# Expert rows written to DRAM by indirect DMA, a ring of nine weight buffers, and the modulation of both layers in layer one

## The chip, the core and the metric

The kernel runs on one core of one Trainium2 chip. The metric is device microseconds of one execution, the median of several runs. All data are float32. TensorE (PE in the profile) runs at one of two granted clock levels: a granted clock of 1.00 is 2.4 GHz, 0.50 is 1.2 GHz.

## What is computed

One inference step of a two-layer backbone for 128 context tokens and 256 latent tokens, with a model width of 1024. The conditioning vectors give six modulation vectors per layer and stream (shift, scale and gate, for the mixer and for the experts). Each layer:

```python
mod = (silu(cond) @ w_mod + b_mod).reshape(6, 1024)
h = rms_norm(x, norm_mix) * (1 + mod[1]) + mod[0]
proj = h @ w_in                      # three head groups: short conv, attention, RWKV-7
x = x + mod[2] * (mixed(proj) @ w_out)
h2 = rms_norm(x, norm_ffn) * (1 + mod[4]) + mod[3]
# hierarchical MoE: best group of 4, best 2 of its 8 experts, 32 experts in all
y[t] = sum over the 2 chosen experts e of weight[t, e] * ((silu(h2 @ w1[e]) * (h2 @ w3[e])) @ w2[e])
x = x + mod[5] * y
```

At the end one more RMS norm. With 384 tokens and two experts each there are 768 (token, expert) rows in a layer, 24 for an expert on average.

## The kernel before

Layout: tokens are columns and the 1024 channels are 8 chunks of 128 partitions. One loop runs over the two layers, and inside it a loop over rounds of 64 slots for each expert; the trace holds one round per layer.

**Mixer** (`mixer_stage`, L400). SP issues every weight load from one queue, in program order, with waits in between. The modulation weights of a layer are 24 pieces of 1 MB, in two buffers (`mod_stream`): piece n+2 is issued by `load_mod` (L802) once TensorE has used piece n. Two pieces make a block of 512 outputs (`mod_piece`, matmuls in L430); a block is then copied by VectorE (L1079), turned by TensorE (`mod_turn`, L441) and summed (L1085). The first eight pieces stand ahead of the input projection. The other sixteen stand between its eleven column groups, two behind each of the first eight (`mod_with`, `MOD_WITH`). `project` (L481) computes one half of a column group: 16 matmul passes of 385 columns. TensorE executes in program order, so whatever it waits for in `mod_with` holds up the next `project`.

At the end of the mixer, when the last two chunks of the mixed heads are ready (`mix_ready`), SP loads the first three weight units of the experts (L822, L826). Meanwhile the last output projection (L669), the second norm, the router and the slot positions are computed, and the normed tokens are stored row by row to DRAM (`h2_rows`, L838). Then the block ends, SP clears all semaphores in a block of its own, and the number of rounds is read.

**Experts** (`experts_round`, L1478). Experts come in pairs (16 pairs), 64 slots each. A weight unit is one matrix of one expert, 2 MB; a pair has six, in six buffers, each loaded again when the pair's own step has used it (L1521). For a pair TensorE does: `up` (L1592, 64 passes of 512 columns for w1 and w3), in it the slot-to-token index (L1559), then `scatter` (L1599) of the pair before: a matmul with the one-hot weights that adds the results of 128 slots onto all 384 tokens, in banks 0 to 5, which are kept as sums through the round. Then the turned one-hot weights (L1616), the turned hidden rows (L1620), `down` (L1607, 32 passes) and the turned token rows of the next pair (L1567). GpSimd gathers these rows from `h2_rows` by an indirect DMA of 128 rows of 4 KB (L1725). After the last pair three weight units are loaded once more, for a possible next round.

**Between and behind.** The next mixer begins with adding the sums to the residual, from PSUM (`add_experts`, L394), and the same is done ahead of the final norm (`close_sums`, `final_stage`). Before the first mixer a block of its own loads the tokens and the constants (L1776 to L1783) and clears the sum banks.

Of the kernel before, what the change touches and what calls it, by code (L numbers as in the profile page):

```python
# [23 lines left out]
I32 = mybir.dt.int32  # L24
# [21 lines left out]
MAX_ROUNDS = T // SLOTS  # L46
DECAY = 0.6065306597126334
# [15 lines left out]
for _name, _w in (("ident", P), ("ones", P), ("heads", P), ("before", P), ("swap", P),  # L63
                  ("cos", TS), ("sin", TS), ("att", 2 * P), ("tri", 4 * P), ("level", 2 * LEVELS * P),
                  ("reset", 3 * 129), ("iota", SLOTS), ("rev", EPG), ("eps", 2), ("tokid", TILES)):
    CK[_name] = _n
    _n += _w
# [3 lines left out]
def build(nc, a, o):  # L71

    ctx = ExitStack()
    with ctx:
# [15 lines left out]
        par = sb("par", NPK)  # L90
        nout = sb("nout", KC)
        cond = sb("cond", 2 * KC)
        mod_sb = sb("mod_sb", 96)
        mod = mod_sb[:, :].rearrange("p (j s) -> p j s", s=2)
        gains = sb("gains", 32)
        gain = gains[:, :].rearrange("p (n c s) -> p n c s", n=2, s=2)
        posm = sb("posm", TILES * N_EXP)
        wall = sb("wall", TILES * N_EXP)
        rounds_i = sb("rounds_i", 1, I32)
        slot_tok = sb("slot_tok", 1, I32)  # L100
        h2_rows = nc.dram_tensor("h2_rows", (T, D), F32, kind="Internal").ap()
        AR_N = 45080
# [7 lines left out]
        def pk(name, i=0, n=1):  # L110
            return par[:, PK[name] + i:PK[name] + i + n]
# [14 lines left out]
        Pm, PT = arena[:, h_at:h_at + 768], arena[:, h_at + 768:h_at + 1536]  # L126
        slab = take(8 * W).rearrange("p (c w) -> p c w", c=8)
# [9 lines left out]
        mix_at = at[0]  # L137
        mixT = take(KC * T).rearrange("p (c t) -> p c t", c=KC)
# [4 lines left out]
        R_, K_, V_ = take(T), take(T), take(T)  # L143
# [17 lines left out]
        zeros = X_.rearrange("p i q -> p (i q)")[:, 0:512]  # L161
# [16 lines left out]
        rtw = take(KC * 36).rearrange("p (c e) -> p c e", c=KC)  # L178
# [6 lines left out]
        r_at = [h_at + KC * T + 24]  # L185

        def rt(n):
# [10 lines left out]
        oh2 = rt(TILES * EPG).rearrange("p (t e) -> p t e", t=TILES)  # L198
        tw = rt(TILES * EPG).rearrange("p (t e) -> p t e", t=TILES)
# [3 lines left out]
        assert r_at[0] <= mix_at  # L203

        unit = [arena[:, i * 4096:(i + 1) * 4096] for i in range(2)]
        h2tok = arena[:, mix_at:mix_at + TILES * D].rearrange("p (t d) -> p t d", t=TILES)
        assert 2 * 4096 <= mix_at  # L210
        m_at = mix_at + TILES * D
        unit = [arena[:, m_at + i * 4096:m_at + (i + 1) * 4096] for i in (2, 3)] + unit + \
               [arena[:, m_at + i * 4096:m_at + (i + 1) * 4096] for i in (0, 1)]
        m_at += 4 * 4096
        e_at = [2 * 4096]

        def moe(n):
            if e_at[0] + n > mix_at and e_at[0] < m_at:
                e_at[0] = m_at
            e_at[0] += n  # L220
            assert e_at[0] <= AR_N
            return arena[:, e_at[0] - n:e_at[0]]

        Sel = moe(TILES * P).rearrange("p (t j s) -> p t j s", t=TILES, j=2)
        Wsel = moe(TILES * P).rearrange("p (t j s) -> p t j s", t=TILES, j=2)
        WselT = moe(T)
# [3 lines left out]
        yg = moe(D)  # L230
        xtok = moe(D)

        pos3 = posm[:, :].rearrange("p (t e) -> p t e", t=TILES)
        wall3 = wall[:, :].rearrange("p (t e) -> p t e", t=TILES)
# [70 lines left out]
        N_MOD, N_IN, N_OUT = 2 * 6 * D // MC, IN_W // UC, D // UC  # L305
        SUM_BANKS = KC * T // 512
# [4 lines left out]
        MOD_WITH = [[m for m in range(N_MOD1, N_MOD) if (m - N_MOD1) * 8 // (N_MOD - N_MOD1) == k] for k in range(N_IN)]  # L311
# [66 lines left out]
        def segments(c):  # L378

            at_, out = c * T, []  # L380
            while at_ < (c + 1) * T:
                n = min((c + 1) * T, (at_ // 512 + 1) * 512) - at_
                out.append((at_ // 512, at_ % 512, at_ - c * T, n))
                at_ += n
            return out

        def add_experts(done=None):

            for c in range(KC):
                for bk, col, t0, n in segments(c):  # L390
                    for st, (cols, _) in enumerate(STREAMS):
                        lo, hi = max(t0, cols.start), min(t0 + n, cols.stop)
                        if lo < hi:
                            ins = nc.vector.scalar_tensor_tensor(  # L394
                                xT[:, c, lo:hi], bank[bk][:, col + lo - t0:col + hi - t0],
                                mod[:, 40 + c, st:st + 1], xT[:, c, lo:hi], ALU.mult, ALU.add)
                if done:
                    done(ins)

        def mixer_stage(layer):  # L400

            pr = PsumTurns(list(range(5)))
            att_turn = [0]

# [7 lines left out]
            with nc.Block() as block:  # L412
                @block.tensor
                def _(pe):
                    mm = nc.tensor.matmul

                    def piece(n):
                        pe.wait_ge(sem(f"piece_loaded{n % 2}"), 16 * (n // 2 + 1))
                        return stream[n % 2]
# [34 lines left out]
                    pe.wait_ge(sem("cond_ready"), 2)  # L454
                    for n in range(N_MOD1):
                        mod_piece(n)
                        if n % 2 and n > 1:
                            mod_turn(n // 2 - 1)
                        if 1 <= n <= KC // 2:
                            pe.wait_ge(sem("sq_ready"), 2 * n)  # L460
# [1018 lines left out]

# [430 lines left out]
```

## Time and profile before

| | us |
|---|---|
| median of three runs | 2093.07 (2092.96 to 2096.77) |
| profiled execution, device time | 2098.63 |
| its span, first to last instruction | 2096.7 |
| TensorE busy | 1846.2 (88%) |
| VectorE / ScalarE / GpSimd busy | 644.5 / 372.6 / 138.6 |
| moved by DMA | 524.84 MB, 250 GB/s over the span |
| mean granted clock | 0.957 |

Times below count from the start of the span. A timeline row reads: start, duration of the whole group, engine and line, operation, result<-operands, tile, number of instructions, and in brackets how long the engine stood idle before it and what ended that. A float32 matmul shows as two passes. "SPq" and "POOL" rows of DMAs show the issue, not the transfer. In a queue row the last figure is the share of the time of 16 DMA engines in that stretch.

### The profile page before, as it was taken

Reading aid. Unit: us, or ns where it says so; the run is one execution under the profiler, and the core shown is the slowest. Engines: PE = TensorE matmul, PEld = TensorE weight load, DVE = VectorE, ACT = ScalarE, POOL = GpSimd, SP = SyncE. Lnnn points to the kernel's source line nnn. Section 1 sums busy time; section 2 is a strip of 40 time slices with the busy share of each in tenths; the row PEclk is TensorE's granted clock in tenths of the full one; section 3 lists DMA queues with packets and bytes.
Section 4 is the critical chain, followed back from the end, with each engine's and each line's share of the span. In section 5 each row is a group of like instructions: output and inputs, shape, how many; then the busy total and the mean of one; then the engine's idle time right before and its main releaser. Section 6 shows DMA issues by size and latency. Waiting matters only on the chain. (4 is left out here: it accounts for less than half of the span.)

```text
span 2096.7 us, 25042 instructions
## 1 busy us (share of the span) xinstructions
PE 1846.2 (88%) x9550; PEld 1042.7 (50%) x9550; DVE 644.5 (31%) x1549; ACT 372.6 (18%) x733; POOL 138.6 (7%) x230
## 2 busy tenths in 40 slices
PE   6998878898899999999789997889879999999994
PEld 2556666675444344344335565677553434434432
DVE  3034566536111111111132436674441111111112
ACT  1022233212110111111021123331121011111101
POOL 0002021120000000000000111122000000000000
PEclk8999899999899999999979999999989999999997
DMA  8551000014899999999676300000259999999992
GB/s 331 211 217 49 16 1 1 16 36 156 352 425 427 425 428 425 418 420 425 269 292 250 141 36 16 1 1 16 90 208 417 427 426 427 426 424 423 420 422 104
DMA packets 48833, 524.84 MB, mean 250 GB/s; under 512 B 5616, under 2 KB 7664, under 8 KB 13808
## 3 DMA queue, kind: packets, MB, share of 16 engines
q1 hardware_dynamic: 42272, 506.00, 58.3%
q0 software_dynamic: 4320, 15.73, 1.9%
q10 hardware_dynamic: 2160, 2.03, 0.3%
q8 instruction: 50, 0.82, 0.2%
q14 instruction: 31, 0.25, 0.0%
HBM read 518.50 MB, written 5.24 MB: 250 GB/s over the span
## 5 line engine op out<-in xcount | busy, mean ns | idle before, releaser
L1592 PE MATMUL bank<-arena 128*64 128x512 f32 x2048 | 453.9, 595 | 0.9
L1592 PEld LDWEIGHTS bank<-arena 128*64 128x64 f32 x2048 | 146.0, 136 | 261.7 <-issue 261.0
L1607 PE MATMUL bank<-arena 128*64 128x512 f32 x1024 | 226.8, 594 | 22.5 <-ACT arena L1705 20.8
L481 PE MATMUL bank<-arena 128*128 128x385 f32 x704 | 239.7, 498 | 2.5 <-ACT arena L910 2.5
L481 PEld LDWEIGHTS bank<-arena 128*128 128x128 f32 x704 | 135.0, 195 | 94.8 <-issue 9.5
L1599 PE MATMUL bank<-arena 128*128 128x384 f32 (+2 forms) x768 | 174.9, 384 | 1.7 <-DVE arena L1689 1.7
L871 POOL TENSOR_TENSOR arena<-arena,const 128x256 f32<-128x256 f32 x168 | 108.1, 668 | 741.3 <-DVE arena L1227 573.0
L1599 PEld LDWEIGHTS bank<-arena 128*128 128x128 f32 x768 | 123.3, 190 | 59.8 <-issue 27.8
L1607 PEld LDWEIGHTS bank<-arena 128*64 128x64 f32 x1024 | 71.8, 135 | 157.0 <-issue 128.9
L1249 DVE TENSOR_TENSOR arena<-arena,bank 128x384 f32<-128x384 f32 x176 | 95.9, 553 | 146.7 <-PE bank L572 113.3
L1685 DVE TENSOR_TENSOR arena<-arena,bank 128x512 f32<-128x512 f32 x32 | 22.0, 688 | 337.9 <-PE bank L1592 337.9
L1689 DVE COPY arena<-bank 128x512 f32<-128x512 f32 x32 | 22.1, 692 | 250.8 <-PE bank L1607 250.8
L1725 POOL DMA_INDIRECT arena<-h_rows,slot_tok x30 | 28.4, 946 | 1044.3 <-DVE slot_tok L1682 1044.3
L572 PE MATMUL bank<-arena 128*128 128x128 f32 x480 | 74.2, 295 | 25.0 <-ACT arena L991 25.0
L574 PE MATMUL bank<-arena 128*128 128x128 f32 x576 | 85.9, 290 | 3.8 <-ACT arena L991 3.8
L669 PE MATMUL bank<-arena 128*128 128x384 f32 x256 | 86.2, 488 | 3.0 <-DVE arena L1399 3.0
L430 PE MATMUL bank<-arena 128*32 128x512 f32 x384 | 52.2, 648 | 37.1 <-DMA arena<-in_w_mod 26.9
L557 PE MATMUL bank<-arena 128*128 128x128 f32 x576 | 78.1, 280 | 6.7 <-issue 6.6
L1712 ACT ACTIVATE arena<-bank 128x384 f32<-128x384 f32 x32 | 15.7, 491 | 373.2 <-PE bank L1616 373.2
L1710 ACT ACTIVATE arena<-bank 128x512 f32<-128x512 f32 x32 | 19.1, 598 | 349.5 <-PE bank L1592 349.5
L574 PEld LDWEIGHTS bank<-arena 128*128 128x128 f32 x576 | 77.7, 205 | 4.7 <-ACT arena L991 4.2
L572 PEld LDWEIGHTS bank<-arena 128*128 128x128 f32 x480 | 64.9, 205 | 28.6 <-ACT arena L991 28.4
(251 smaller groups left out, 1808.2 us busy)
## 6 DMA issues: line engine op xcount, KB each, us to landing
arena<-in_exp_w SPq DMA_DIRECT2D x198, 2048.0 KB, 14.9
arena<-in_w_mod SPq DMA_DIRECT2D x48, 1024.0 KB, 5.3
arena<-in_w_in SPq DMA_DIRECT2D x22, 1024.0 KB, 8.3
arena<-in_w_out SPq DMA_DIRECT2D x8, 768.0 KB, 4.3
h_rows<-arena SPq DMA_DIRECT2D x2, 1536.0 KB, 5.3
const<-in_const SPq DMA_DIRECT2D x1, 2088.0 KB, 10.6
arena<-in_w_out_rw SPq DMA_DIRECT2D x2, 1024.0 KB, 4.7
x_sb<-in_xT SPq DMA_DIRECT2D x1, 1536.0 KB, 6.7
```

What stands on the lines that cost most here:

```text
L430: last = mm(mod_bank[0][32 * g:32 * g + 32, :], scond[:, 4 * second + g, :], mod_stream[n % 2][:, g, :], start=not second, stop=bool(second))
L481: last = mm(b[:, 0:W - 2], w[:, c, j * P:(j + 1) * P], hT[:, c, 1:W - 1], start=(c == 0), stop=(c == KC - 1))
L557: last = mm(b[:, (i % 3) * P:(i % 3 + 1) * P], Nl[lev % 2][:, i, :], X_[:, i, :] if lev else ident, start=True, stop=True)
L572: last = mm(o_, XT[:, i, :], T1[:, i, :], start=True, stop=True)
L574: last = mm(o_, T1[:, i, :], XT[:, i, :], start=True, stop=True)
L669: last = mm(b[:, 0:T], w[:, c - chunks[0], col:col + P], mixT[:, c, :], start=(c == chunks[0]), stop=(c == chunks[-1]))
L871: ins = g.tensor_tensor(Nl[lev % 2][:, 2 * t:2 * t + 2, :], G[:, t, :, 0, 0, :], m, ALU.mult)
L1249: L.free(tt(x[:, ii, :], x[:, ii, :], b[:, 0:T].rearrange("p (i q) -> p i q", i=3), ALU.add), pr, name, hold=False)
L1592: last = mm(b[HALF[j], :], Xg[:, c, j, :], unit[2 * m + j][:, c * DE:(c + 1) * DE], start=(c == 0), stop=(c == KC - 1))
L1599: mm(bank[bk][:, col:col + n], yg[:, c * P:(c + 1) * P], WselT[:, t0:t0 + n], start=False, stop=True, skip_group_check=True)
L1607: last = mm(b[HALF[j], :], hidT[:, f_, j, :], unit[4 + j][:, lo:lo + 512], start=(f_ == 0), stop=(f_ == FC - 1))
L1725: nc.gpsimd.indirect_dma_start(xtok, None, h2_rows[:, :], bass.IndirectOffsetOnAxis(ap=slot_tok[:, 0:1], axis=0))\
```

## The change

- Expert results are no longer added up in PSUM. They are scaled by their weight on the way out of PSUM, and GpSimd writes each slot's row to one of two rows of its token in DRAM (`y_rows`) by an indirect DMA; an empty slot has an index out of bounds and moves nothing. The `scatter` matmuls and the turned one-hot weights go. The two rows of every token are read back, added and turned (`read_rows`, `turn_rows`, `add_experts`) at the start of the next mixer and ahead of the final norm. `h2_rows` is stored twice, so that either row index of a token finds it.
- Weight units go through nine buffers in turn. The first nine of a layer are loaded from `mix_ready` on; unit n waits for the step that used unit n-9. A unit is loaded again for a further round only by an indirect DMA whose indices are out of bounds in the first round (`hold_again`). The first two input pieces of the next mixer are loaded behind the last unit.
- All 48 modulation pieces of both layers are used in the first layer: 8 ahead of the projection, and 40 behind the first eight column groups, six and four in turn. The second layer has none.
- The block ahead of the first mixer goes; its loads stand behind the first two modulation pieces. Layers and pairs are written out instead of looped; the mixer's semaphores are cleared inside the round.

```diff
-        MOD_WITH = [[m for m in range(N_MOD1, N_MOD) if (m - N_MOD1) * 8 // (N_MOD - N_MOD1) == k] for k in range(N_IN)]
+        MOD_WITH = [[m for m in range(N_MOD1, N_MOD) if (m - N_MOD1) // 2 * 8 // ((N_MOD - N_MOD1) // 2) == k] for k in range(N_IN)]
...
+        def read_rows(sp):
+            for t in range(TILES):
+                for k in range(2):
+                    sp.dma_start(ytok[:, t, k, :], y_rows[k * T + t * P:k * T + (t + 1) * P, :])\
+                      .then_inc(sem(f"rows_read{t}"), 16)
+
+        def turn_rows(pe, pr):
+            for t in range(TILES):
+                pe.wait_ge(sem("rows_added"), t + 1)
+                for half in range(2):
+                    b = pr.open(pe, f"rows{t}_{half}")
+                    for i in range(4):
+                        last = nc.tensor.transpose(b[:, i * P:(i + 1) * P],
+                                                   ytok[:, t, 0, (4 * half + i) * P:(4 * half + i + 1) * P], ident)
+                    pr.close(last, f"rows{t}_{half}")
...
+            add(0)
+            residual(0)
+            add(1)
+            add(2)
+            residual(1)
+            residual(2)
...
                     def mod_with(k):
-                        for m in MOD_WITH[k]:
+                        for m in MOD_WITH[k] if first else ():
...
-                    for n in range(N_MOD1):
-                        load_mod(n)
+                    if first:
+                        for n in range(N_MOD1):
+                            load_mod(n)
+                            if n == 1:
+                                sp.dma_start(x_sb[:, :], a["xT"]).then_inc(sem("x_loaded"), 16)
+                                sp.dma_start(const[:, :], a["const"]).then_inc(sem("const_loaded"), 16)
+                                sp.dma_start(nout[:, :], a["nout"]).then_inc(sem("stored"), 16)
+                    else:
+                        for s_ in range(HELD):
+                            sp.sem_clear(sem(f"held{s_}"))
+                        read_rows(sp)
                     for m, u in enumerate(IN_ORDER):
                         load(m, a["w_in"][bass.ds(layer * (N_IN * P) + u * P, P), :])
-                        for n in MOD_WITH[m]:
+                        for n in MOD_WITH[m - 1] if first and m else ():
                             load_mod(n)
...
+                    sp.wait_ge(sem("mix_ready"), 2)
+                    def hold(n):
+                        i, m, j = n // 6, n % 6 // 2, n % 2
+                        src = a[("exp_w1", "exp_w3", "exp_w2")[m]][bass.ds((layer * N_EXP + i * 2 + j) * P, P), :]
+                        sp.dma_start(unit[n], src).then_inc(sem(f"held{n}"), 16)
+                    for n in range(HELD - 1):
+                        hold(n)
+                    pr.filled(sp, f"out1_{KC - 1}")
+                    hold(HELD - 1)
                     pr.copied(sp, f"htok{TILES - 1}1")
-                    sp.dma_start(h2_rows.rearrange("(t p) d -> p t d", p=P), h2tok).then_inc(sem("h2_stored"), 16)
+                    for k in range(2):
+                        sp.dma_start(h2_rows[k * T:(k + 1) * T, :].rearrange("(t p) d -> p t d", p=P), h2tok)\
+                          .then_inc(sem("h2_stored"), 16)
+                    sp.wait_ge(sem("h2_stored"), 32)
...
+                    for n in range(HELD, 6 * PAIRS):
+                        i, m, j = n // 6, n % 6 // 2, n % 2
+                        before = n - HELD
+                        sp.wait_ge(sem(used[before % 6 // 2]), before // 6 + 1)
+                        sp.dma_start(unit[n % HELD], a[names[m]][bass.ds((layer * N_EXP + i * 2 + j) * P, P), :])\
+                          .then_inc(sem(f"x_unit{n % HELD}"), 16)
+                    if layer + 1 < DEPTH:
+                        sp.wait_ge(sem("x_down"), PAIRS - 1)
+                        for k in range(2):
+                            src = a["w_in"][bass.ds((layer + 1) * (N_IN * P) + IN_ORDER[k] * P, P), :]
+                            sp.dma_start(stream[k], src.rearrange("p (c n) -> p c n", c=KC)).then_inc(sem("x_next"), 16)
...
+                    index(0)
+                    turned(0)
+                    index(1)
+                    for i in range(PAIRS):
+                        up(i)
+                        turned(i + 1)
+                        turn_hidden(i)
+                        index(i + 2)
+                        down(i)
...
+                    hold_again(0)
+                    hold_again(1)
+                    gather(0)
+                    for n in range(2, HELD):
+                        hold_again(n)
+                    gather(1)
+                    for i in range(PAIRS):
+                        gather(i + 2)
+                        pool.wait_ge(sem("x_y0"), i + 1)
+                        pool.wait_ge(sem("x_y1"), i + 1)
+                        if i:
+                            pool.wait_ge(sem("x_put"), 16 * i)
+                        g.indirect_dma_start(y_rows[:, :], bass.IndirectOffsetOnAxis(ap=slot_idx[i % 3][:, 0:1], axis=0),
+                                             yg[i % 2], None, bounds_check=2 * T - 1, oob_is_err=False)\
+                            .then_inc(sem("x_put"), 16)
+                    pool.wait_ge(sem("x_put"), 16 * PAIRS)
```

## Rows read from the trace of the kernel before

**Rows 1.** The page, 40 slices of 52.4 us: busy tenths of the DMA engines.

```profile
DMA  8551000014899999999676300000259999999992
```

**Rows 2.** Timeline of TensorE, one pair of the first layer's experts.

```profile
596.53 3.66 PE L1592 MATMUL bank<-arena 128*64 128x512 f32 x16
611.57 5.47 PE L1599 MATMUL bank<-arena 128*128 128x384 f32 x24
619.29 7.09 PE L1607 MATMUL bank<-arena 128*64 128x512 f32 x32 [0.69 <-ACT arena L1705]
627.86 3.66 PE L1592 MATMUL bank<-arena 128*64 128x512 f32 x16
```

**Rows 3.** DMA queues in 560 to 1030 us: packets, MB, share.

```profile
q1 hardware_dynamic: 13086, 190.54, 95.8%
q0 software_dynamic: 2016, 7.34, 4.0%
q8 instruction: 3, 0.05, 0.0%
```

**Rows 4.** Weight units of the experts (L1521), 480 to 700 us, from issue.

```profile
DMA to landing us min/median/max: 8.6/17.8/23.7
```

**Rows 5.** Timeline of TensorE, the second column group of the first projection.

```profile
72.18 1.92 PE L430 MATMUL bank<-arena 128*32 128x512 f32 x16
74.03 0.66 PE L441 MATMUL bank<-const,arena 128*128 128x128 f32 x4
74.53 10.52 PE L481 MATMUL bank<-arena 128*128 128x385 f32 x32
```

**Rows 6.** Timeline of TensorE, modulation ahead of the first projection, and its first group.

```profile
32.71 1.06 PE L430 MATMUL bank<-arena 128*32 128x512 f32 x8 [0.53 <-DMA arena<-in_w_mod]
38.77 1.07 PE L430 MATMUL bank<-arena 128*32 128x512 f32 x8 [1.85 <-DMA arena<-in_w_mod]
46.37 13.48 PE L481 MATMUL bank<-arena 128*128 128x385 f32 x32 [1.27 <-ACT arena L910]
```

**Rows 7.** Modulation pieces (L802), 22 to 42 us, from issue.

```profile
DMA to landing us min/median/max: 4.7/4.7/7.7
```

**Rows 8.** Stretches: us, busy PE PEld DVE ACT POOL, granted clock, DMA share, GB/s.

```profile
26.70:41.20 14.50, 10.71 (x60) 3.63 (x60) 5.59 (x8) 1.86 (x2) 0.00 (x0) 1.00 0.91 344
1070.20:1073.40 3.20, 1.07 (x8) 0.16 (x8) 3.17 (x2) 0.00 (x0) 0.00 (x0) 0.90 1.01 415
```

**Rows 9.** Timeline, second layer: end of the experts, sums, norm, first projection.

```profile
1030.03 5.44 PE L1599 MATMUL bank<-arena 128*128 128x384 f32 x24 [0.88 <-DVE arena L1689]
1044.37 5.54 DVE L394 SCALAR_TENSOR_TENSOR x_sb<-bank,mod_sb,x_sb 128x128 f32<-128x128 f32 x18 [14.38 <-issue]
1069.84 2.55 DVE L1094 RECIPROCAL arena<-arena 128x384 f32<-128x384 f32 x1
1072.42 3.43 DVE L1112 TENSOR_TENSOR arena<-x_sb,arena 128x1536 f32<-128x1536 f32 x2
1079.42 12.37 PE L481 MATMUL bank<-arena 128*128 128x385 f32 x32 [1.27 <-ACT arena L910]
```

**Rows 10.** Timeline of SP and TensorE, first layer: mixer's end, start of the experts.

```profile
484.39 0.87 SPq L822 DMA_DIRECT2D arena<-in_exp_w  x2
518.47 0.39 SPq L838 DMA_DIRECT2D h_rows<-arena  x1
530.89 8.47 PE L1552 MATMUL bank<-arena 128*128 128x128 f32 x48 [7.86 <-DVE arena L1662]
```

**Rows 11.** Indirect gathers (L1725), whole run: time on GpSimd (ns), then issue to landing.

```profile
L1725 POOL DMA_INDIRECT arena<-h_rows,slot_tok x30: 937/939/1112, 544.2 to 2001.8; - x30
DMA to landing us min/median/max: 6.0/10.8/12.0
```

**Rows 12.** Timeline, second layer: held units issued; sums added ahead of the final norm.

```profile
1511.92 0.87 SPq L822 DMA_DIRECT2D arena<-in_exp_w  x2
2068.14 5.54 DVE L394 SCALAR_TENSOR_TENSOR x_sb<-bank,mod_sb,x_sb 128x128 f32<-128x128 f32 x18 [11.27 <-PEq L238]
```

More of the change, by code:

```diff
@@ L793, in load @@
                         dst = stream[n % 2] if dst is None else dst
+                        if n < 2 and not first:
+                            return
                         sp.dma_start(dst, src.rearrange("p (c n) -> p c n", c=dst.shape[1]))\
@@ L1602, in down @@
-                    def down(i, half, last_pair):
-                        b = bB if half else bA
-                        for f_ in range(FC):
-                            for j in range(2):
-                                lo = f_ * D + half * 512
-                                last = mm(b[HALF[j], :], hidT[:, f_, j, :], unit[4 + j][:, lo:lo + 512],
-                                          start=(f_ == 0), stop=(f_ == FC - 1))
-                        last.then_inc(sem("b_filled" if half else "a_filled"), 1)
@@ L1651, in _ @@
-                    scatter()
+                        for half, b in enumerate((D0, D1)):
+                            if i:
+                                pe.wait_ge(sem(("x_y0", "x_y1")[half]), i)
+                            for f_ in range(FC):
+                                for j in range(2):
+                                    lo = f_ * D + half * 512
+                                    last = mm(b[HALF[j], :], hidT[:, f_, j, :], unit[(6 * i + 4 + j) % HELD][:, lo:lo + 512],
+                                              start=(f_ == 0), stop=(f_ == FC - 1))
+                            last.then_inc(sem(("x_down0", "x_down")[half]), 1)
@@ L1729, in _, with final_stage @@
+                    pool.wait_ge(sem("x_put"), 16 * PAIRS)
                     pool.dma_reset()
-        def close_sums():
+        def final_stage():
+            pr = PsumTurns(list(range(8)))
             with nc.Block() as block:
+                @block.tensor
+                def _(pe):
+                    turn_rows(pe, pr)
+                    b = pr.open(pe, "ss")
+                    for c in range(KC):
+                        pe.wait_ge(sem("sq_ready"), c + 1)
+                        last = nc.tensor.matmul(b[:, 0:T], ones, sq[:, c, :], start=(c == 0), stop=(c == KC - 1))
+                    pr.close(last, "ss")
+                @block.scalar
+                def _(act):
+                    L = Lane(act, "act_steps")
+                    f = nc.scalar.activation
+                    for c in range(KC):
+                        if c % 4 == 3:
+                            pr.copied(act, f"rows{TILES - 1}_{c // 4}")
+                        else:
+                            act.wait_ge(sem("residual_ready"), c - c // 4 + 1)
+                        L.sig(f(sq[:, c, :], xT[:, c, :], ACT.Square), "sq_ready", hold=False)
+                    b = pr.filled(act, "ss")
+                    L.free(f(ss[:, :], b[:, 0:T], ACT.Sqrt, bias=ck("eps", 1), scale=1.0 / D), pr, "ss", hold=False)
@@ L1798, in build @@
-        with nc.Fori(0, DEPTH) as layer:
+                    read_rows(sp)
+                    for k in range(4):
+                        sp.wait_ge(sem("y_ready"), 2 * k + 2)
+                        sp.dma_start(o["yT"][:, 2 * k * T:2 * (k + 1) * T],
+                                     h2T[:, 2 * k:2 * k + 2, :].rearrange("p c t -> p (c t)")).then_inc(sem("stored"), 16)
+                    sp.wait_ge(sem("stored"), 64)
+        for layer in range(DEPTH):
             mixer_stage(layer)
-            clear(list(sems.values()))
+            mixer_sems = [s for name, s in sems.items() if name[:2] != "x_" and name[:4] != "held"]
```

652 lines of the change are left out of this document (309 added, 343 removed).

## The prediction

> **What bounds the kernel now.** First the 40 slices of the page: the DMA engines are full in slices 11 to 19 and 30 to 39, the two layers' expert stages, about half busy at the start of each mixer, and nearly idle in between [rows 1]. So there are two kinds of stage, and I looked at each for the wait that ends last. In the expert stage the timeline of TensorE shows one pair from 596.53 to 627.86, 31.33 us, and in it nearly no gap: up, scatter, down and the turns follow each other [rows 2]. The queue rows of the same stage show the DMA engines full as well: 95.8% for weights and 4.0% for gathers over 470 us [rows 3], and a unit lands 17.8 us after its issue where its own transfer takes 5, so about two and a half units always wait in the queue [rows 4]. The stage is therefore bound twice, by TensorE at 31.3 us a pair and by the DMA engines just below it. From the queue rows: weights move at 190.54 MB / (0.958 x 470 us) = 423 GB/s, so a unit of 2.097 MB costs 4.96 us; indirect rows at 7.34 / (0.040 x 470) = 390 GB/s. In the projection of the mixer TensorE alone sets the pace: two modulation pieces, 1.92 us, a turn, 0.66, then 10.52 us of `project` without a gap [rows 5].
>
> **The change, part by part.**
>
> *Modulation, first layer.* Before, each of eight column groups has one pair of pieces behind it, which lands during the 10.5 us of `project`; it costs only 1.92 + 0.66 = 2.6 us [rows 5]. After it there are 20 pairs in the same eight places, three and two in turn, still through two buffers. Only the first pair of a place can land during `project`. Every further pair must be issued when its buffers come free, and TensorE stands in order in front of it. What that costs is seen ahead of the first projection, where pieces follow each other in this way: the same point of two successive pairs is 38.77 - 32.71 = 6.06 us apart [rows 6], which is a landing of 4.7 us [rows 7], 1.07 of matmul and some 0.3 of issue. Twelve further pairs: 12 x 6.06 = 73 us. On top, the first pair of a place is used at once and not staggered, so its successors land one transfer (1.05 MB / 423 GB/s = 2.48 us) apart behind it, and a place takes 16.4 or 10.4 us instead of 14.7 or 8.6: 8 x 1.8 = 15. Sum **+88** (73 to 92). Nothing hides it: what is late next is the `project` behind it, and the whole mixer behind that.
>
> The Trainium skill, page "DMA: Bandwidth & Descriptors", section "Bandwidth", has a measured table for loads issued from GpSimd in which 1 MB takes 6.15 us. With that a pair could not come in under 12.3 us, the twelve would cost 75 us more, and the time would be near 2220. The rows of this kernel, whose loads SP issues, show 4.7 us with the landing included [rows 7], and the sum goes by them.
>
> *TensorE's clock in these places.* The granted clock stayed at 1.00 where the engine was busy for 10.71 of 14.50 us, and had begun to fall at 0.90 after 1.07 busy in 3.20 [rows 8]. Between the first and second pair it will stand idle for some 3.5 us, which is nearer to the second row. If the clock falls, a group like that of 46.37 takes 13.48 us instead of 10.5 [rows 5, 6], eight times 2.9, and a piece 1.93 instead of 1.07, 12 x 0.86: 34 us in all. If it does not, nothing. I take half, **+17** (0 to 34).
>
> *Start of the first layer.* The block of its own goes. But tokens and constants (3.7 MB) now stand on the same queue behind the first two pieces: 5.8 MB and the small loads at 423 GB/s plus 2.2 us of latency (4.7 - 2.48) is 18; the second pair lands by 23.5, two more at 6.06 put piece 6 at 33.5. From piece 6 to the projection it was 46.37 - 38.77 = 7.6 [rows 6]; so 41 instead of 46.4: **-5** (-9 to -2).
>
> *Second layer, places.* No modulation: 8 x 2.6 = **-20.5**, with TensorE the bound there before and after.
>
> *Second layer, start.* Before, from the sums to the first projection 1079.42 - 1044.37 = 35.0 us [rows 9]. After: six row loads, 3.1 MB, land from 4.7 to 10 us; adding, turning and 24 residual operations of 0.31 us (5.54 for 18) end near 18; square, sum and root 2.7; then 2.55 and 3.43 [rows 9], and the first modulated chunk: 27.5. **-7.5** (-12 to -3).
>
> *Expert stage, first layer.* Without scatter (5.47) and the turned one-hot weights (about 0.5) TensorE needs 31.33 - 6 = 25.4 us a pair [rows 2]. The DMA engines need 6 x 4.96 = 29.8 and, for 48 filled slots on average, 48 x 4 KB x 2 = 0.39 MB at 390 GB/s = 1.0: 30.8. So scatter's 5.5 us a pair are worth almost nothing: the DMA engines become the only bound, half a microsecond lower. What counts is the bytes of the stage and when they start. Held units: from 484.39 [rows 10], 2.2 of latency, 9 x 4.96 = 44.6, and behind them in the same queue the two stores of 1.57 MB, 7.4: 538.6. The block waits for these stores, so the mixer now ends with the loads. Before, store, block end and clearing took from 518.47 to 530.89 [rows 10], of which the store some 5.9, so 6.5 of handover; without the clearing 4: the round starts at 542.6. Then slot choice, index, two `hold_again` and the gather on GpSimd at 0.94 us each [rows 11] and its landing (6.0 is the shortest [rows 11]; 5 with empty queues), turns, and the first half of `up` partly at the low clock: 21 us until a buffer comes free, and 2.2 of latency. All this time, 538.6 to 565.8, the DMA engines have nothing to do. Then 87 units, 431 us, and 6.3 MB of rows, 16: 1013. Behind the last unit `down` 7.1 [rows 2], scaling 0.7, the last put 5, handover and clearing 6: the next mixer starts at 1032 instead of 1044.4 [rows 9]: **-12.5** (-24 to -2). The reloads that go (3 units) ended before scatter did, and were worth nothing.
>
> *Expert stage, second layer, and the end.* The same 541.5 us from the first held unit, 1511.92 [rows 12], plus 5 of handover: 2058.4 instead of 2068.14. The final stage grows from 2096.7 - 2068.1 = 28.6 to 31, since rows must be read and turned first, though the store goes out in four parts. **-7.5** (-19 to +3).
>
> Sum: +88 + 17 - 5 - 20.5 - 7.5 - 12.5 - 7.5 = **+52 us**. The profiled execution took 2098.63, its span 2096.7 and 1.9 around it; the median is 5.6 lower, and the difference is put on the median: 2093 + 52 = **2145**. With the terms' bounds against each other this case spans 2115 to 2178. A change below 0.2% (4.2 us) can't be told from none.
>
> **Rivals.**
>
> *The DMA engines carry more than they showed (faster).* TensorE set the pace of 31.3 us, so 423 GB/s may be what was asked for and not what can be had. For: some units land after 8.6 us [rows 4]. Against: the share is full and 2.5 units queue. It ends faster from 447 - 28 = 419 us for the 188.8 MB, that is from 450 GB/s; at 455 both stages together save 65: 2080. Chance 0.15.
>
> *The modulation waits cost only their bytes.* If the fixed part of a landing overlaps and the clock holds, a pair costs 2 x 2.48 = 4.96: 12 x 4.96 = 59 instead of 105, 2099. Against it stand the 6.06 us [rows 6], which already have two loads in flight. Chance 0.13, spread over the three signs.
>
> *GpSimd is the new wait (slower still).* `hold_again` names rows of 16 KB, and the first gathers stand behind nine of them. If one takes 4 us and not the 0.94 of a 4 KB row [rows 11], gather 0 is 6 us later and gather 1 holds up the first `down` and the loads behind it by 8: 14 a layer, 2173. Chance 0.09.
>
> *Unrolled code.* Before, the pairs are a loop, and three blocks of 16 KB of code were loaded in 470 us [rows 3]; after, each pair is new code, about one such block for TensorE, through the same full engines. If each stopped TensorE for a loaded gather's 10.8 us [rows 11], a pair took 25.4 + 10.8 = 36.2 and not 30.8: 32 x 5.4 = 173 more, 2318. The mixer is such code, and runs without gaps [rows 5]. Chance 0.03. The Trainium skill, page "Runtime: NRT & Kernel Launch", section "Instruction fetch mechanics", says that an engine fetches the next page while it executes the current one and that this is mostly hidden, and that taken branches break it. By that the rival falls away; no row here shows it under full queues.
>
> **How the numbers follow.** Forecast 0.60, slower; the rivals as given. Faster 0.15 + 0.03 = 0.18; same 0.05; slower 0.60 + 0.05 + 0.09 + 0.03 = 0.77. The range reaches from the first rival to the third and its bounds: 2080 to 2185.
>
> **What would show it.** Right: in the first layer waits of TensorE for modulation loads, absent before in the places, of some 100 us together; TensorE waiting for units in every pair, period near 30.8 us; DMA idle for some 25 us at the start of each round; a second mixer without modulation that begins some 7 us faster. Wrong: places without waits, an expert stage below 530 us from the first held unit to the next mixer, or TensorE without waits in the pairs.

## The result and the profile after

| | before | after |
|---|---|---|
| median of the runs, us | 2093.87 (2092.96 to 2096.77) | 2156.93 (2151.83 to 2162.73) |
| span of the profiled execution, us | 2096.7 | 2153.1 |
| mean granted clock | 0.957 | 0.922 |

The ratio is 1.0293, with an interval of 1.0268 to 1.0318: 3% slower. The forecast was 2145 us, slower, with a range of 2080 to 2185. Between the profiled spans the change is 56.4 us, between the medians 63; the sum had +52. The two differ because the profiled execution of before lies above its median (2098.63 us of device time) and that of the changed kernel below its own (2154.92).

The two costliest waits, from the page of the changed kernel, and the row of the modulation pieces from the same table of before:

```profile
L1625 PE MATMUL bank<-arena 128*64 128x512 f32 x2048 | 476.8, 621 | 150.9 <-DMA arena<-in_exp_w 150.9
...
L463 PE MATMUL bank<-arena 128*32 128x512 f32 x384 | 68.8, 813 | 68.5 <-DMA arena<-in_w_mod 62.2
```

```profile
L430 PE MATMUL bank<-arena 128*32 128x512 f32 x384 | 52.2, 648 | 37.1 <-DMA arena<-in_w_mod 26.9 <-ACT arena L891 10.3
```

TensorE waits in two groups more than before: 150.9 us in `up` (L1625) for weight units, where it had 0.9 us of idle time in all, and 62.2 us in `mod_piece` (L463) for modulation loads, where it had 26.9, all of them ahead of the two first projections. Only the second makes the kernel slower. The first replaces work: `scatter` has gone, and TensorE stands where it used to add.

**First layer, places.** The same groups of TensorE from the first projection to the end of the places, first before, then after: instructions, busy us and mean ns, idle us ahead of them.

```profile
L481 PE MATMUL bank<-arena 128*128 128x385 f32 x256 | 87.4, 500 | 1.3 <-ACT arena L910 1.3
L430 PE MATMUL bank<-arena 128*32 128x512 f32 x128 | 15.4, 598 | 0.0
L441 PE MATMUL bank<-const,arena 128*128 128x128 f32 x36 | 5.8, 285 | 1.5 <-DVE mod_sb L1085 1.5
```

```profile
L519 PE MATMUL bank<-arena 128*128 128x385 f32 x256 | 89.4, 509 | 1.4 <-DVE arena L1161 1.4
L463 PE MATMUL bank<-arena 128*32 128x512 f32 x320 | 56.8, 810 | 46.8 <-DMA arena<-in_w_mod 46.8
L474 PE MATMUL bank<-const,arena 128*128 128x128 f32 x80 | 17.7, 361 | 0.0
```

The three rows grow by 2.0, by 41.4 busy and 46.8 idle, and by 11.9: 102 us. They can be split. At the durations of before, the 192 further piece matmuls take 192 x 15.4/128 = 23.1 and the 44 further turns 44 x 5.8/36 = 7.1: 30 us of plain work, which would be there without any wait. 46.8 is waiting. The rest, 25, is the same work at a lower clock, 18 in the pieces, 5 in the turns and 2 in `project`: a piece's matmul has a mean of 810 ns instead of 598.

One four-piece place of the changed kernel, then a part of a six-piece place, from the timeline of TensorE:

```profile
86.10 1.92 PE L463 MATMUL bank<-arena 128*32 128x512 f32 x16
...
92.11 1.31 PE L463 MATMUL bank<-arena 128*32 128x512 f32 x8 [3.50 <-DMA arena<-in_w_mod]
...
97.38 11.63 PE L519 MATMUL bank<-arena 128*128 128x385 f32 x32
108.95 1.92 PE L463 MATMUL bank<-arena 128*32 128x512 f32 x16
...
114.85 1.07 PE L463 MATMUL bank<-arena 128*32 128x512 f32 x8 [3.39 <-DMA arena<-in_w_mod]
...
120.77 1.93 PE L463 MATMUL bank<-arena 128*32 128x512 f32 x8 [0.43 <-DMA arena<-in_w_mod]
```

The first pair is there, as in [rows 5]; the next one makes TensorE wait 3.5 us, and successive pairs stand 6.0, 5.9 and 5.9 us apart. (Of the twelve further pairs nine stand 5.9 to 6.0 apart, and three 6.7 to 8.1.) Behind the waits the same work takes longer: a piece 1.93 us instead of 1.07, and this `project` 11.63 instead of 10.52. In this stretch of a six-piece place (columns as in [rows 8]) the granted clock was 0.65, between the two levels:

```profile
217.00:235.00 18.00, 12.06 (x60) 3.03 (x60) 4.03 (x9) 1.90 (x3) 0.00 (x0) 0.65 0.80 307
```

**Experts.** The stretch 700 to 1050 us, DMA queues and then busy time (same columns):

```profile
q1 hardware_dynamic: 9897, 144.22, 96.9%
q0 software_dynamic: 3450, 4.86, 3.8%
q8 instruction: 11, 0.18, 0.2%
```

```profile
700.00:1050.00 350.00, 277.16 (x1324) 114.07 (x1320) 44.26 (x122) 21.35 (x34) 23.35 (x23) 0.98 1.01 427
```

The DMA engines are as full as in [rows 3], at 427 GB/s; TensorE is now busy for only 277 of 350 us. `up` in the timeline of TensorE, where a row holds both halves of it (x64) or the first half (x32):

```profile
677.72 13.90 PE L1625 MATMUL bank<-arena 128*64 128x512 f32 x64
700.94 13.90 PE L1625 MATMUL bank<-arena 128*64 128x512 f32 x64
...
753.07 7.09 PE L1625 MATMUL bank<-arena 128*64 128x512 f32 x32 [3.24 <-DMA arena<-in_exp_w]
...
1093.60 7.09 PE L1625 MATMUL bank<-arena 128*64 128x512 f32 x32 [2.59 <-DMA arena<-in_exp_w]
```

The first three of the sixteen pairs run without a wait, 23.2 us from `up` to `up`, on units that had landed before. From the fifth pair to the last, 753.07 to 1093.60, eleven pairs take 31.0 us each, with a wait for units in each of them; [rows 2] had 31.3.

The stage as a whole, by SP's issues (the rows that answer to [rows 10] and [rows 12]):

```profile
583.19 10.91 SPq L873 DMA_DIRECT2D arena<-in_exp_w  x9
...
661.57 419.88 SPq L1571 DMA_DIRECT2D arena<-in_exp_w  x87
1131.63 3.05 SPq L382 DMA_DIRECT2D arena<-y_rows  x6
1575.94 10.92 SPq L873 DMA_DIRECT2D arena<-in_exp_w  x9
...
2122.05 2.90 SPq L382 DMA_DIRECT2D arena<-y_rows  x6
```

Held units are issued at 583.19 and 1575.94; the ring first turns at 661.57; the rows are read at 1131.63 and 2122.05. From these points the stages of the experiments are compared.

### The profile page after: what moved, and what is told of

The parts are those of the page before. It is cut to its first block and busy times, and to the rows that moved or that the text cites. A ratio compares the mean times of both kernels' runs of the same rounds, so it can differ in the third digit from the quotient of the medians.

```text
span 2153.1 us, 21913 instructions
## 1 busy us (share of the span) xinstructions
PE 1682.2 (78%) x8630; PEld 942.9 (44%) x8630; DVE 641.8 (30%) x1577; ACT 323.8 (15%) x678; POOL 194.5 (9%) x283
## 3 DMA queue, kind: packets, MB, share of 16 engines
q1 hardware_dynamic: 44368, 502.87, 56.4%
## 5 line engine op out<-in xcount | busy, mean ns | idle before, releaser
L1625 PE MATMUL bank<-arena 128*64 128x512 f32 x2048 | 476.8, 621 | 150.9 <-DMA arena<-in_exp_w 150.9
L1625 PEld LDWEIGHTS bank<-arena 128*64 128x64 f32 x2048 | 171.1, 142 | 453.8 <-issue 453.8
L1647 PE MATMUL bank<-arena 128*64 128x512 f32 x1024 | 226.8, 595 | 22.8 <-DMA arena<-in_exp_w 17.9
L519 PEld LDWEIGHTS bank<-arena 128*128 128x128 f32 x704 | 137.4, 198 | 104.2 <-issue 18.5
L1647 PEld LDWEIGHTS bank<-arena 128*64 128x64 f32 x1024 | 79.9, 137 | 145.0 <-issue 119.3
L463 PE MATMUL bank<-arena 128*32 128x512 f32 x384 | 68.8, 813 | 68.5 <-DMA arena<-in_w_mod 62.2
L1719 DVE TENSOR_SCALAR arena<-bank,slot_w 128x512 f32<-128x512 f32 x32 | 24.0, 751 | 203.8 <-PE bank L1647 203.8
L1767 POOL DMA_INDIRECT arena<-h_rows,slot_idx x32 | 32.5, 1014 | 566.1 <-DVE slot_w L1684 564.9
L612 PEld LDWEIGHTS bank<-arena 128*128 128x128 f32 x576 | 77.2, 204 | 4.7 <-ACT arena L1050 4.2
L1743 ACT ACTIVATE arena<-bank 128x512 f32<-128x512 f32 x32 | 19.1, 598 | 397.9 <-PE bank L1625 397.9
L595 PEld LDWEIGHTS bank<-arena 128*128 128x128 f32 x576 | 71.1, 191 | 15.3 <-issue 7.6
L610 PEld LDWEIGHTS bank<-arena 128*128 128x128 f32 x480 | 64.4, 204 | 28.6 <-ACT arena L1050 28.4
L1139 DVE COPY arena<-bank 128x512 f32<-128x512 f32 x24 | 16.6, 690 | 189.1 <-PE bank L463 189.1
L1735 ACT ACTIVATE arena<-bank 128x512 f32<-128x512 f32 x32 | 19.2, 599 | 304.9 <-PE bank L1611 304.9
```

The lines of the kernel that those rows point to most:

```text
L463: last = mm(mod_bank[0][32 * g:32 * g + 32, :], scond[:, 4 * second + g, :], mod_stream[n % 2][:, g, :], start=not second, stop=bool(second))
L519: last = mm(b[:, 0:W - 2], w[:, c, j * P:(j + 1) * P], hT[:, c, 1:W - 1], start=(c == 0), stop=(c == KC - 1))
L595: last = mm(b[:, (i % 3) * P:(i % 3 + 1) * P], Nl[lev % 2][:, i, :], X_[:, i, :] if lev else ident, start=True, stop=True)
L610: last = mm(o_, XT[:, i, :], T1[:, i, :], start=True, stop=True)
L612: last = mm(o_, T1[:, i, :], XT[:, i, :], start=True, stop=True)
L1625: last = mm(b[HALF[j], :], Xg[:, c, j, :], unit[(6 * i + 2 * m + j) % HELD][:, c * DE:(c + 1) * DE], start=(c == 0), stop=(c == KC - 1))
```

## The experiments

My theory was the working of the prediction: the modulation's waits, with the clock that falls in them, are the loss; the experts' stage gains a little, because it becomes bound by the DMA engines alone and starts late. The rivals: the bytes or the pair of buffers set the pace whatever the order; the experts' new form costs something of its own; GpSimd's order is a wait; the DMA engines could carry more.

**Modulation of each layer in its own layer.** One part undone; the rows that are read back move to another place in the arena, so that layer 2's modulation buffers are free.

```diff
-        N_MOD, N_IN, N_OUT = DEPTH * 2 * 6 * D // MC, IN_W // UC, D // UC
+        N_MOD, N_IN, N_OUT = 2 * 6 * D // MC, IN_W // UC, D // UC
...
                         read_rows(sp)
+                        for n in range(N_MOD1):
+                            load_mod(n)
...
-                        for n in MOD_WITH[m - 1] if first and m else ():
+                        for n in MOD_WITH[m - 1] if m else ():
```

> The changed kernel with one part undone: each layer computes its own modulation again (24 pieces: 8 ahead of the projection, 16 in the eight places); rows, ring and indirect writes stay. Theory (the modulation move is the whole loss, the other parts gain): the places of layer 1 go from 118 us back to 21 (-97), those of layer 2 grow by 20.5, the start of layer 2 by about 7 (rows 7.4 us, four pairs at 6.06, then 7.6 to the projection: 39 instead of 31.7). Sum -69 against 2157: 2088 us, 5 below the kernel before. Rival 1, the eight pieces of layer 2 don't hide behind its rows at all and its start grows by 24: 2105. Rival 2, the loss lies in the experts' new form and not in the modulation: the time stays above 2130.

Measured: 2084.74 us, 0.9946 of before (0.9926 to 0.9965). Without the moved modulation the change is faster than the kernel before. The timeline of TensorE, first projection, end of the places (L554), and in the second layer the rows' turning and the first projection:

```profile
45.56 13.56 PE L517 MATMUL bank<-arena 128*128 128x385 f32 x32 [1.45 <-DVE arena L1161]
156.88 0.82 PE L554 MATMUL bank<-const,arena 128*128 128x128 f32 x6
...
1040.96 3.67 PE L392 MATMUL bank<-const,arena 128*128 128x128 f32 x16 [2.53 <-DVE arena L402]
...
1075.59 12.26 PE L517 MATMUL bank<-arena 128*128 128x385 f32 x32 [1.45 <-DVE arena L1161]
```

The stretch is 156.88 - 45.56 = 111.3 us. In the changed kernel it is 213.4 (row below), so the 24 further pieces cost 102 there, the same figure as from the groups. Layer 2's start grew to 47 us and not 39: TensorE turns the rows first, so no modulation buffer came free before 1044.6. That the loss is in the experts is refuted.

```profile
45.29 12.14 PE L519 MATMUL bank<-arena 128*128 128x385 f32 x32 [1.45 <-DVE arena L1161]
258.69 1.49 PE L556 MATMUL bank<-const,arena 128*128 128x128 f32 x6
```

**The same pieces in sixteen places.**

```diff
-                        project(u, 0)
-                        project(u, 1)
-                        mod_with(k)
+                        for j in range(2):
+                            project(u, j)
+                            mod_with(2 * k + j)
```

> The changed kernel with the same 40 pieces in layer 1's places, but spread over sixteen places (behind each half of a column group) instead of eight: 1, 1, 1, 2 pairs instead of 3 and 2. Same bytes, same two buffers, same order. Theory (what costs is a landing that no projection covers): a single pair lands during the 5.25 us of a half group up to some 2 us, only the four second pairs wait in full: 31 us of plain work for the 12 more pairs, 16 to 30 of waits, clock near 1.00, places 82 instead of 118: 2121 us (2107 to 2137). Rival (the pair of buffers, or the bytes, set a pace that position can't change): 2157, within 5.

Measured: 2119.55 us, 1.0109 (1.0085 to 1.0133), 37 less than the changed kernel. The pieces' group in the stretch of the places:

```profile
L462 PE MATMUL bank<-arena 128*32 128x512 f32 x320 | 44.4, 649 | 29.4 <-DMA arena<-in_w_mod 29.4
```

Waits fall from 46.8 to 29.4 and work from 56.8 to 44.4, with the same bytes and buffers. Position alone is worth more than half of the 63 us; the rival falls. The granted clock of these places rose from 0.83 to 0.91, not to near 1.00 as expected.

**TensorE kept busy in the waits.**

```diff
                         for m in MOD_WITH[k] if first else ():
+                            if m % 2 == 0 and m > MOD_WITH[k][0]:
+                                for c in range(6):
+                                    mm(bank[5][:, 0:W - 2], ident, hT[:, c, 1:W - 1], start=True, stop=True)
                             mod_piece(m)
```

> The changed kernel with six matmuls of 128x385 into an unused bank ahead of each second and third pair of a place, so that TensorE works (2.9 us) where it waited some 3.5 us for the load. Theory (the lower clock is part of the cost, term +17): the granted clock of the places rises from 0.65 to 0.81 to near 1.00, pieces take 1.07 instead of 1.93, a place 16.4 instead of 18.2 and 10.4 instead of 11.3 to 12.8: -14, 2143 us (2133 to 2152). Rival (the landing alone sets the pace, the clock runs in its shadow): 2157 within 4, or up to 10 more where the added matmuls outlast the landing.

Measured: 2141.28 us, 1.0232 (1.0199 to 1.0265), 16 less. The pieces' group, the stretch of the places (the same columns as above), and from the timeline of TensorE the first projection and the end of the places:

```profile
L463 PE MATMUL bank<-arena 128*32 128x512 f32 x320 | 40.6, 601 | 11.7 <-DMA arena<-in_w_mod 11.5
```

```profile
46.00:248.00 202.00, 188.04 (x823) 93.51 (x825) 39.11 (x100) 20.27 (x40) 0.00 (x0) 0.99 0.64 248
```

```profile
46.72 12.37 PE L522 MATMUL bank<-arena 128*128 128x385 f32 x32 [1.45 <-DVE arena L1164]
...
246.70 0.82 PE L559 MATMUL bank<-const,arena 128*128 128x128 f32 x6
```

With 48.7 us of useless matmuls added the kernel is faster: the clock is 0.99, a piece's matmul is back at 601 ns, and `project` at 10.5. So the clock was a cost of its own, and did not all run in the shadow of the landings. How large a cost is bounded and not fixed: the places take 246.70 - 46.72 = 200.0 us, 13.4 less than in the changed kernel, and not 25 less. Part of the slower work had filled time in which TensorE would have waited; and the useless matmuls outlast some landings, as the further pairs stand 6.8 us apart in the mean, for 6.2. The clock cost between 13 and 25 us, and the places at a full clock between 77 and 89 more than the 111.3 of the kernel with its own modulation.

**The h2 stores ahead of the last two held units.** GpSimd's reload of those two then waits for them.

```diff
-                    for n in range(HELD - 1):
+                    for n in range(7):
                         hold(n)
-                    pr.filled(sp, f"out1_{KC - 1}")
-                    hold(HELD - 1)
                     pr.copied(sp, f"htok{TILES - 1}1")
...
+                    for n in range(7, HELD):
+                        hold(n)
                     sp.wait_ge(sem("h2_stored"), 32)
```

> The changed kernel with the two stores of h2 ahead of the last two held units in SP's queue instead of behind all nine. Theory (the experts' stage is bound by the DMA engines, so what counts is when its round starts and the transfers go on): the store lands at about 630 instead of 637.5, the round starts 7.5 us earlier, the DMA engines stand idle for some 17 us instead of 25 before the ring turns, in both layers: -15, 2142 us. Rival 1 (the ring's start is set by the route or by the first pairs on TensorE, not by the stores): within 4 of 2157. Rival 2 (the round's first gathers meet the two late units in the queues, and all that is won is lost there): within 4 as well, but with a round that starts 7 us earlier.

Measured: 2151.67 us, 1.026 (1.0236 to 1.0284). SP's issues:

```profile
592.94 3.96 SPq L873 DMA_DIRECT2D arena<-in_exp_w  x7
...
664.81 421.38 SPq L1571 DMA_DIRECT2D arena<-in_exp_w  x87
1133.69 3.04 SPq L382 DMA_DIRECT2D arena<-y_rows  x6
```

From the held units to the ring's first turn it is 71.9 us instead of 78.4, and to the rows 540.8 instead of 548.4. The second layer's stage is 538.9 instead of 546.1. So the stages give 15, as expected; but the first mixer, in which nothing was changed ahead of the held units, took 592.94 instead of 583.19, and the time shows 5. The kernel run once more, below, takes this up.

**Half of `up` left out.** Four of eight chunks, so the rows are not the whole product.

```diff
-                            for c in range(KC):
+                            for c in range(KC // 2):
```

> The changed kernel with half of `up` left out (four of eight chunks), so that the experts' rows are not the whole product: TensorE needs 7 us less per pair, the bytes stay. Theory (the DMA engines are the only bound of the experts' stage, 30.4 us a pair): the pairs keep their period; only the first buffer comes free some 4 us earlier in each layer, and the last pair is shorter by up to 4: -8 to -16, 2141 to 2149 us. Rival (TensorE still sets the pace in part of the pairs): 7 us for each such pair, 140 us less if it were ten in each layer, up to 448.

Measured: 2150.86 us, 1.0257 (1.024 to 1.0274), 10 less than the changed kernel on the same chip (2161.09, below). TensorE's timeline, one pair, and the same stretch as above:

```profile
910.95 5.35 PE L1625 MATMUL bank<-arena 128*64 128x512 f32 x16 [3.88 <-DMA arena<-in_exp_w]
...
941.62 3.65 PE L1625 MATMUL bank<-arena 128*64 128x512 f32 x16 [1.41 <-DMA arena<-in_exp_w]
```

```profile
700.00:1050.00 350.00, 233.26 (x918) 92.06 (x918) 43.47 (x121) 20.71 (x33) 22.29 (x22) 0.80 1.01 427
```

With 7 us less to do, a pair still takes 30.7 (30.8 in the mean from the fifth to the last, for 31.0), and the bytes still flow at 427 GB/s. TensorE sets the pace of none of these pairs, and 427 is what can be had here, not what was asked for.

**Without `hold_again`.** The reload of held units for a second round is left out.

```diff
-                            pe.wait_ge(sem(f"x_again{n}"), 16)
...
-                    hold_again(0)
-                    hold_again(1)
                     gather(0)
-                    for n in range(2, HELD):
-                        hold_again(n)
                     gather(1)
```

> The changed kernel without the nine `hold_again` of a round: it leaves out the reloading of the held units for a second round, which the routing of this input does not have. Theory (one costs GpSimd 1.0 us and hides, but for the two ahead of the first gather): the first gather is issued some 2 us earlier, the stage begins 2 us earlier in each layer: -3, 2154 us (2150 to 2156). Rival 3 of the forecast (GpSimd's order is a wait of its own): 14 a layer, 2129.

Measured: 2161.94 us, 1.0324 (1.0301 to 1.0347): no difference from the changed kernel on the same chip. The first gather, in GpSimd's timeline, is at 644.77, in the changed kernel at 646.68, and the stages are 2.6 and 1.0 shorter (table). That is no more than a stage moves without an edit: in the kernel with TensorE kept busy, whose experts are unchanged, layer 1's is 2.9 shorter. So the expected 3 us are not shown, and GpSimd as a new wait of 14 us a layer is refuted.

**The changed kernel once more.**

> The changed kernel itself once more, beside the other three: what stays the same and what moves from one profile to the next. Expected: 2157 us within 5; the experts' stages within 1 us of 547.9 and 546.1, since the DMA engines set them; the mixers within some 10 us of 583 and 445, since TensorE's granted clock sets part of them (in e3_store_ahead the mixer, in which nothing is changed ahead of the held units, took 592.9).

Measured: 2161.09 us, 1.0303 (1.0285 to 1.0321). TensorE and SP, the same points as above:

```profile
45.41 2.91 PE L519 MATMUL bank<-arena 128*128 128x385 f32 x4 [1.45 <-DVE arena L1161]
...
264.32 1.49 PE L556 MATMUL bank<-const,arena 128*128 128x128 f32 x6
```

The same code took 218.9 us for the places and not 213.4, and reached the held units at 591.19. So the first mixer differs by 8 us between two executions of one kernel, and the 592.94 of the store kernel need not be its doing. The chip does not explain it: half of `up` and the kernel without `hold_again`, with the same first mixer and on the chip of this run, reached that point at 588.7 and 583.1. The experts' stages came out within half a microsecond. All kernels, from SP's issues (held units in layer 1 and 2; stage from there to the rows):

| kernel | held, layer 1 | stage 1 | held, layer 2 | stage 2 | time |
|---|---|---|---|---|---|
| changed kernel | 583.2 | 548.4 | 1575.9 | 546.1 | 2156.9 |
| the same once more | 591.2 | 548.0 | 1585.5 | 546.2 | 2161.1 |
| own modulation | 480.3 | 548.7 | 1507.5 | 546.3 | 2084.7 |
| sixteen places | 550.5 | 548.6 | 1543.2 | 546.4 | 2119.6 |
| TensorE kept busy | 570.0 | 545.5 | 1557.0 | 546.8 | 2141.3 |
| stores ahead | 592.9 | 540.8 | 1580.2 | 538.9 | 2151.7 |
| half of `up` | 588.7 | 544.1 | 1579.4 | 540.5 | 2150.9 |
| without `hold_again` | 583.1 | 545.8 | 1575.7 | 545.2 | 2161.9 |
| best (next; its rows stand behind two pieces) | 479.0 | 540.6 | 1495.6 | 539.0 | 2064.9 |

**A version that beats both.** Own modulation and stores ahead, and in layer 2 the first pair of pieces ahead of the rows:

```diff
                         for n in range(N_MOD1):
                             load_mod(n)
+                            if n == 1:
+                                read_rows(sp)
```

> The changed kernel with each layer's own modulation (as in e1_own_mod), in layer 2 the first pair of pieces ahead of the rows in SP's queue, on TensorE and on VectorE, and the h2 stores ahead of the last two held units (as in e3_store_ahead). Theory: from 2085 the start of layer 2 gets 9 us shorter (47.2 to 38, since pieces 2 and 3 no longer wait until the rows are turned), and each experts' stage 7.5: 2061 us (2054 to 2070). Rival (the first pair in the queue delays the rows by as much as it gains, and the earlier round is lost in the mixer's clock): 2078 or more.

Measured: 2064.9 us, 0.985 of before (0.9833 to 0.9866). Against the kernel with its own modulation the stages give 8.1 and 7.3, in the time too. From the rows to the held units the second mixer gave 2.6 where 9 were expected: by this kernel's own order pieces 2 and 3 again stood behind the turning of rows on TensorE,

```profile
1036.49 3.68 PE L392 MATMUL bank<-const,arena 128*128 128x128 f32 x16 [2.53 <-DVE arena L402]
1040.10 2.18 PE L463 MATMUL bank<-arena 128*32 128x512 f32 x16
...
1061.90 10.49 PE L517 MATMUL bank<-arena 128*128 128x385 f32 x23 [1.44 <-DVE arena L1159]
```

without a wait for a load, so it was TensorE's order and not the queue that held back the pairs behind them.

## Why the prediction was right, and where it was off

| term, us | forecast | found |
|---|---|---|
| modulation places, work and waits | +88 | +77 to +89 |
| clock in the places | +17 | +25 to +13 |
| start of layer 1 | -5 | -1.1 |
| layer 2, places | -20.5 | -19.4 |
| layer 2, start | -7.5 | -3.3 |
| experts, layer 1 | -12.5 | -12.1 |
| experts, layer 2, and the end | -7.5 | -7.6 |
| sum | +52 | +58.6 |

The first two rows are 102 together. The span grew by 56.4; the 2 us between stand in the rest of the first mixer. Against +52 the sum is off by 6.6: 3.9 and 4.2 at the starts of the two layers and 1.1 in layer 2's places, less 2.9 in the places of layer 1.

**Modulation.** The step held: a further pair costs a landing, in nine of twelve cases 5.9 to 6.0 us apart, as in [rows 6]. The Trainium skill, page "DMA: Bandwidth & Descriptors", section "Bandwidth", gives 6.15 us for 1 MB loaded from GpSimd; an estimate from it, one load behind the other, is 12.3 us for a pair. This case's loads from SP do not bear that out: in the places no two successive pairs stand more than 8.1 apart. The places of 10.4 and 16.4 us hold too: with the clock at 0.99 (TensorE kept busy) they took 9.9 to 11.9 and 16.2 to 17.4, the useless matmuls included.

The clock's 13 to 25 us lie inside its 0 to 34, but its make-up was wrong, and that the sum fits is in part luck. Of the 34 I had 23 in `project`, eight times a slow group, and 10 in the pieces. By the groups above `project` grew by 2.0 in all, and the pieces and turns by 18 and 5. Also, I named waits of some 100 us as the sign of being right. TensorE waited 46.8 in the places; the rest of the 102 is plain work, 30, and slower work, 25.

That waits cost only their bytes, 4.96 a pair and 2099, is refuted: twelve pairs cost 102, 8.5 each.

**Start of layer 1.** I left out that with the tokens late the channel sums stand between the pieces. Timeline of TensorE:

```profile
27.16 3.14 PE L483 MATMUL bank<-arena,const 128*128 128x384 f32 x8
30.23 1.07 PE L463 MATMUL bank<-arena 128*32 128x512 f32 x8
31.22 2.85 PE L483 MATMUL bank<-arena,const 128*128 128x384 f32 x8
...
36.08 1.06 PE L463 MATMUL bank<-arena 128*32 128x512 f32 x8 [0.42 <-DMA arena<-in_w_mod]
```

Six microseconds of sums put piece 6 at 36.1 instead of 33.5, and piece 7, whose load waits for piece 5, 3.8 behind it. The term was -1.1, outside my -9 to -2.

**Start of layer 2.** The rows came as forecast: the residual (L411) ended 18.6 us after the start, for 18. What I mis-sized is the step behind it, 2.7 for square, sum and root. Timelines of ScalarE, VectorE and TensorE, in order of time:

```profile
1131.08 0.34 ACTq L941 DMA_DIRECT2D arena<-in_w1a  x1
...
1145.47 4.22 DVE L411 SCALAR_TENSOR_TENSOR x_sb<-bank,mod,x_sb 128x128 f32<-128x128 f32 x16
1148.59 5.40 PE L483 MATMUL bank<-arena,const 128*128 128x384 f32 x16 [0.77 <-ACT arena L951]
...
1154.07 1.28 ACT L956 ACT_TABLE_LOAD   x1 [2.73 <-PE bank L483]
...
1162.81 3.55 PE L519 MATMUL bank<-arena 128*128 128x385 f32 x5 [8.83 <-DVE arena L1161]
```

The sixteen passes of the sums alone take 5.40, and they stand by themselves now, with no pieces of modulation to lie between. Behind them ScalarE loads a table for the root, 1.28, and from the first sum to the end of the root it is 7.4 us, 6.3 of them behind the residual. From start to projection it is 1162.81 - 1131.08 = 31.7, against 35.0 [rows 9].

**Layer 2, places.** From the first projection to the held units 1575.94 - 1162.81 = 413.1, before 432.5 [rows 9, 12].

**Experts.** The steps held. Stage 1 is 1131.08 - 583.19 = 547.9 against 560.0 [rows 9, 10], stage 2 546.1 against 556.2 [rows 12], the end 2153.1 - 2122.05 = 31.05 for the 31 forecast. The DMA engines were idle from about 637.5 to 663 at the start of the round, 25 us for 27; a pair took 31.0 in the mean for 30.8. So the removed `scatter`, 5.5 us a pair, became a wait for units. One sign was worded too widely: TensorE does not wait in every pair, since the first three of a layer run on units already landed, at 23.2 us for the 25.4 that I had for TensorE alone. The rival of more than 450 GB/s is refuted by the half `up`.

Unrolled code fell too: 11 packets of the instruction queue, 0.18 MB, came in 350 us, and of TensorE's 73 us of idle time in that stretch 71 are waits for units and 1.5 for VectorE. The Trainium skill, "Runtime: NRT & Kernel Launch", section "Instruction fetch mechanics", says that the cost of going from one block of code to the next is mostly hidden; the trace agrees.

## What to carry to other kernels

- A load that is used in program order costs what of its landing no work covers, so count the places that can cover one and put one load behind each; eight pairs that were covered cost 19.4 us in layer 2's places, and the twelve that were moved cost 102 where only a first pair was covered. Spreading them took back a third. Split what an added step costs into plain work, wait and clock: a better order takes from the last two (waits from 46.8 to 29.4, a piece's matmul from 810 to 649 ns), and leaves the first.
- Removing work from an engine is worth only the distance to the next bound: read the other engine's share in the same stretch first. In a stage that the DMA engines bind, look at what keeps them idle at its start.
- Judge an edit whose effect is a few microseconds by the stage that it touches; the time of the whole had 8 us from another stage in it, and a stage by itself moved by 3.

## What was not expected of the hardware

- One kernel's first mixer differed by 8 us between two profiled executions. In the second, `project` took 94.0 us for the same 256 passes, for 89.4, with nearly the same waits, 47.7 and 46.8; the experts' stages, set by the DMA engines, differed by less than half a microsecond. What makes the clock fall more often in one execution than in another stays open.
- An indirect DMA of which every index is out of bounds costs GpSimd 1.0 us, as much as a gather of rows, and signals 2.1 us after its issue.
- 48.7 us of added matmuls with no use made a kernel 16 us faster.
